# The first norm of a two-block transformer kernel: its modulation columns by pairs of pieces, the tiles behind them, two weight pieces over four PSUM banks

## What is computed

```python
c_act = silu(c)                                   # c: (1, 1024)
mod = (c_act @ w_ada[l] + b_ada[l]).reshape(B, 9, 1024)
sh1, sc1, gt1, ... = mod                          # shift, scale, gate, three times
hn = rms_norm(h, g_ffn1[l]) * (1.0 + sc1) + sh1
h = h + 0.5 * (1.0 + gt1) * swiglu(hn, w_ffn1_in[l], w_ffn1_out[l])
```

## Time and profile before

| | |
|---|---|
| median of 3 runs | 2898.18 us (2896.74 to 2901.25) |
| span of the profiled execution | 2894.2 us |
| the profiled execution's own time | not given apart from its span; the median is 3.98 us above the span |
| TensorE matmul busy | 2752.6 us, 95% of the span |
| VectorE busy | 1490.7 us, 52% |
| ScalarE busy | 967.7 us, 33% |
| GpSimd busy | 199.7 us, 7% |
| first matmul of an "up" piece | at 40.3 us |

### The profile page before, as it was taken

How to read it: one execution, slowest core, us unless ns; L and a number is a source line. 1 busy time by engine, 2 the same in 40 slices (tenths; PEclk the granted TensorE clock), 3 DMA queues, 4 the chain that set the end, 5 groups by cost and what they waited for, 6 DMA issues and landing times.

```text
span 2894.2 us, 42214 instructions
## 1 busy us (share of the span) xinstructions
PE 2752.6 (95%) x17756; PEld 2244.9 (78%) x17756; DVE 1490.7 (52%) x1833; ACT 967.7 (33%) x1471; POOL 199.7 (7%) x271
## 2 busy tenths in 40 slices
PE   6999999898999999999999899999999999968998
PEld 5888877686888878888777777888877777648787
DVE  6565566745555443333357634333365556656534
ACT  3222334523222233222345323222324444422322
POOL 3000000410000000000002300000010000013000
PEclk9999999989999999999999989999999999969999
DMA  7565542102566322232222012232222221100132
GB/s 287 197 226 205 184 160 77 44 18 85 206 205 216 103 94 102 84 112 81 101 73 74 6 59 76 91 103 97 99 89 72 81 73 66 62 1 4 56 102 73
DMA packets 46522, 299.68 MB, mean 104 GB/s; under 512 B 5665, under 2 KB 5793, under 8 KB 18081
## 3 DMA queue, kind: packets, MB, share of 16 engines
q1 hardware_dynamic: 37152, 230.35, 23.3%
q0 software_dynamic: 9216, 67.11, 6.4%
HBM read 295.35 MB, written 2.10 MB: 103 GB/s over the span
## 4 chain that ended last, share of the span: by engine, by line
PE 88%; DVE 8%; ACT 2%; DMA 1%; issue 1%; POOL 0%; SPq 0%; DVEq 0%; ACTq 0%; POOLq 0%
PE ps L920 17%; PE ps L921 17%; PE ps L922 17%; PE ps L1208 5%; PE ps L1209 5%; PE ps L1210 5%; PE ps L1515 2%; PE ps L1516 2%; PE ps L1517 2%; PE ps L2069 1%; PE ps L2053 1%; PE ps L2066 1%; DVE w_lo L897 1%; DMA ada_first<-in_ada 1%; PE ps L1330 1%; DVE tmp L876 1%
## 5 line engine op out<-in xcount | busy, mean ns | idle before, releaser
L920 PE MATMUL ps<-hn_hi,w_hi 128*128 128x512 f32 x1472 | 578.1, 393 | 26.0 <-DVE hn_lo L870 16.7
L921 PE MATMUL ps<-hn_lo,w_hi 128*128 128x512 f32 x1472 | 576.4, 392 | 0.0
L922 PE MATMUL ps<-hn_hi,w_lo 128*128 128x512 f32 x1472 | 575.8, 391 | 0.0
L897 DVE TENSOR_TENSOR w_lo<-w_raw,w_hi 128x2048 fp32r<-128x2048 f32 (+3 forms) x229 | 472.4, 2063 | 181.4 <-ACT w_hi L890 177.9
L890 ACT ACTIVATE w_hi<-w_raw 128x2048 fp32r<-128x2048 f32 (+3 forms) x229 | 394.5, 1723 | 115.8 <-PE ps L1210 97.3
L920 PEld LDWEIGHTS ps<-hn_hi,w_hi 128*128 128x128 f32 x1472 | 278.8, 189 | 87.6 <-issue 28.8
L1208 PE MATMUL ps<-hn_hi,w_hi 128*128 128x512 f32 x776 | 323.3, 417 | 7.8 <-DVE hn_lo L870 4.9
L922 PEld LDWEIGHTS ps<-hn_hi,w_lo 128*128 128x128 f32 x1472 | 278.7, 189 | 58.2
L921 PEld LDWEIGHTS ps<-hn_lo,w_hi 128*128 128x128 f32 x1472 | 279.0, 190 | 57.7
L1209 PE MATMUL ps<-hn_lo,w_hi 128*128 128x512 f32 x776 | 305.8, 394 | 0.0
L1210 PE MATMUL ps<-hn_hi,w_lo 128*128 128x512 f32 x776 | 305.4, 394 | 0.0
(11 more groups left out here) (462 smaller groups left out, 3499.0 us busy)
## 6 DMA issues: line engine op xcount, KB each, us to landing
w_raw<-in_up SPq DMA_DIRECT2D x88, 1024.0 KB, 4.9
ada_w<-in_ada POOLq DMA_DIRECT2D x64, 1024.0 KB, 5.2
w_raw<-in_down SPq DMA_DIRECT2D x64, 704.0 KB, 4.0
w_raw<-in_mix_in SPq DMA_DIRECT2D x20, 1024.0 KB, 4.9
w_raw<-in_dsa_in SPq DMA_DIRECT2D x18, 1024.0 KB, 4.9
w_raw<-in_merge SPq DMA_DIRECT2D x16, 768.0 KB, 4.3
ada_first<-in_ada SPq DMA_DIRECT2D x8, 1024.0 KB, 12.4
w_raw<-in_mix_out SPq DMA_DIRECT2D x8, 1024.0 KB, 5.0
```

The costliest lines, as they stand in the source:

```text
L897: dve.tensor_tensor(w_lo[:, slot, 0:size], w_raw[:, slot, 0:size], w_hi[:, slot, 0:size].bitcast(F32), ALU.subtract).then_inc(w_lo_ready, 1)
L920: pe.matmul(bank, wh, x_hi[:, k], start=(k == 0), stop=False)
L921: pe.matmul(bank, wh, x_lo[:, k], start=False, stop=False)
L922: return pe.matmul(bank, wl, x_hi[:, k], start=False, stop=(k == K - 1))
```

## The change

- **Loads.** x comes in two halves. The weights of piece 0 are issued ahead of the `ada` pieces, those of piece 1 after the first four of them. The `ada` pieces come as pairs: a scale piece, then the shift piece of the same two tiles (4, 0, 5, 1, 6, 2, 7, 3), from the third pair on each after the piece two pairs before. The weights of piece 2 are the next that the loop over weights issues.
- **Sum of squares.** The first norm adds six of its squared tiles on VectorE as the later norms do. The identity matrix has a mark of its own, so the spread no longer waits for the other masks.
- **Columns.** Of each piece, the first column stays one custom instruction on VectorE. For the second, GpSimd multiplies (128 x 1024, both inputs in SBUF), ScalarE sums with a Copy that has an accumulator, and VectorE adds the bias (one column).
- **Tiles.** `norm_gain` is formed column by column, and each tile's L876, `hn_hi` and `hn_lo` follow as soon as its two columns are there. VectorE finishes one tile (`low(j)`) before it goes on.
- **Pieces 0 and 1.** TensorE runs both while the tiles arrive: piece 0 in full for each k, piece 1's two products with `w_hi` from k = 3 on, and piece 1's sixteen products with `w_lo` last. The two pieces are in four banks. Splits: piece 1's inside the norm, piece 2's in step 0.
- **GpSimd.** The six levels of masks go out of `make_masks` into `level_masks`, behind the norm and between the first two later `ada` loads and the rest. Later marks count one higher.
- **Step 0.** The first later `ada` piece is summed after `act_lo`, not ahead of `act_f`.

```diff
-    sp.dma_start(h[:], w["x"]).then_inc(x_loaded, 16)
-    for q in range(ADA_FIRST):
-        if q == ADA_FIRST - 2:
-            sp.dma_start(w_raw[:, 0, 0:WIDE], w["up"]((0, 0), 0)).then_inc(raw_loaded[0], 16)
-        if q >= 4:
-            sp.wait_ge(ada_first_loaded[q % 4], 16)
-        sp.dma_start(ada_first[:, q], w["ada"][q]).then_inc(ada_first_loaded[q % 4], 16)
+    for q in range(X_PARTS):
+        part = slice(q * KD // X_PARTS, (q + 1) * KD // X_PARTS)
+        sp.dma_start(h[:, part], w["x"][:, part]).then_inc(x_loaded[q], 16)
+    sp.dma_start(w_raw[:, 0, 0:WIDE], w["up"]((0, 0), 0)).then_inc(raw_loaded[0], 16)
+    for pair in range(ADA_FIRST // 2):
+        for q in (ADA_FIRST // 2 + pair, pair):
+            if pair >= 2:
+                sp.wait_ge(first_loaded(q), 16)
+            sp.dma_start(ada_first[:, q], w["ada"][q]).then_inc(first_loaded(q), 16)
+        if pair == 1:
+            sp.dma_start(w_raw[:, 1, 0:WIDE], w["up"]((0, 0), 1)).then_inc(raw_loaded[1], 16)
...
-            if isinstance(i, int) and p0 + i == 0:
-                return
-            if not (isinstance(i, int) and p0 + i < 2):
-                sp.wait_ge(w_lo_ready, p0 + i - 1)
+            sp.wait_ge(w_lo_ready, p0 + i - 1)
...
+        elif p0 == 0:
+            steps(sp, n - 2, lambda i, odd: load(i + 2, odd))
...
        select(ident[:], [[-1, P]], 0, 1, ALU.not_equal, 1.0)
+        pool.memset(pool_mark[:], 0.0).then_inc(masks_ready, 1)
...
+    def level_masks(pool):
         for lv in range(1, 7):
...
-    pool.wait_ge(ada_done, ADA_FIRST)
-    load_ada(0, ADA_BEFORE_MIX)
+    pool.wait_ge(c_row_ready, 1)
+    for pair in range(ADA_FIRST // 2):
+        for q in (ADA_FIRST // 2 + pair, pair):
+            pool.wait_ge(first_loaded(q), 16 * (pair // 2 + 1))
+            pool.tensor_tensor(ada_first[:, q, 1], ada_first[:, q, 1], c_row[:], ALU.mult).then_inc(ada_multiplied, 1)
+    pool.wait_ge(hn_ready, KD)
+    load_ada(0, 2)
+    level_masks(pool)
+    load_ada(2, ADA_BEFORE_MIX)
...
+def first_column_dve(dve, own, q):
+    dve.wait_ge(first_loaded(q), 16 * (q % (ADA_FIRST // 2) // 2 + 1))
+    col = 2 * q
+    ws = ada_first[:, q, 0]
+    own(dve.tensor_tensor_reduce(ws, ws, c_row[:], 1.0, b_ada[:, col:col + 1], ALU.mult, ALU.add, mod[:, col:col + 1]))
+def second_column_dve(dve, own, q):
+    half_, pair = (0, q - ADA_FIRST // 2) if q >= ADA_FIRST // 2 else (1, q)
+    dve.wait_ge(ada_done, 2 * pair + half_ + 1)
+    col = 2 * q + 1
+    own(dve.tensor_tensor(mod[:, col:col + 1], mod[:, col:col + 1], b_ada[:, col:col + 1], ALU.add))
+def second_column_act(act, q):
+    half_, pair = (0, q - ADA_FIRST // 2) if q >= ADA_FIRST // 2 else (1, q)
+    act.wait_ge(ada_multiplied, 2 * pair + half_ + 1)
+    col = 2 * q + 1
+    act.activation(ada_first[:, q, 1], ada_first[:, q, 1], ACT.Copy, accum_out=mod[:, col:col + 1]).then_inc(ada_done, 1)
+def first_norm_act(act):
+    shift = mods(0, 0)
+    for j in range(KD):
+        pair, odd = j // 2, j % 2
+        second_column_act(act, ADA_FIRST // 2 + pair if odd == 0 else pair)
+        act.wait_ge(hn_tmp, j + 1)
+        act.activation(hn_hi[:, j], tmp[:, odd], ACT.Identity, bias=shift[:, j:j + 1]).then_inc(hn_hi_ready, 1)
+        if j == 3:
+            split_act(act, (1, 1), WIDE)
+def first_norm_dve(dve, own):
+    gain, shift, scale = gains[:, 0, 0], mods(0, 0), mods(0, 1)
+    def tile_(j):
+        own(dve.scalar_tensor_tensor(norm_gain[:, j:j + 1], scale[:, j:j + 1], 1.0, gain[:, j:j + 1], ALU.add, ALU.mult))
+        if j >= 2:
+            dve.wait_ge(hn_ready, j - 1)
+        dve.scalar_tensor_tensor(tmp[:, j % 2], h[:, j], norm_gain[:, j:j + 1], small[0], ALU.mult,
+                                 ALU.mult).then_inc(hn_tmp, 1)
+    def low(j):
+        dve.wait_ge(hn_hi_ready, j + 1)
+        dve.scalar_tensor_tensor(hn_lo[:, j], tmp[:, j % 2], shift[:, j:j + 1], hn_hi[:, j].bitcast(F32),
+                                 ALU.add, ALU.subtract).then_inc(hn_ready, 1)
+    first = ADA_FIRST // 2
+    for pair in range(first):
+        first_column_dve(dve, own, first + pair)
+        if pair:
+            second_column_dve(dve, own, first + pair - 1)
+            second_column_dve(dve, own, pair - 1)
+            tile_(2 * pair - 1)
+            low(2 * pair - 1)
+        first_column_dve(dve, own, pair)
+        if pair == 0:
+            dve.wait_ge(norm_spread, 1)
+        tile_(2 * pair)
+        low(2 * pair)
+        if pair == 2:
+            split_dve(dve, (1, 1), WIDE)
+    second_column_dve(dve, own, ADA_FIRST - 1)
+    second_column_dve(dve, own, first - 1)
+    tile_(KD - 1)
+    low(KD - 1)
...
+        act.wait_ge(sq_added, SQ_ADDS * n + max(1, j - 2))
...
+            if j % (KD // X_PARTS) == 0:
+                act.wait_ge(x_loaded[j * X_PARTS // KD], 16)
             norm_square(act, 0, j)
-    act.wait_ge(sq_summed, KD + 2 * n)
+    act.wait_ge(sq_summed, 2 * (n + 1))
...
+def first_pieces_pe(pe):
+    def products(p, t, k, low):
+        col = (2 * k + t) * P
+        wh, wl = w_hi[:, p, col:col + P], w_lo[:, p, col:col + P]
+        bank = main[p][t]
+        if low:
+            return pe.matmul(bank, wl, hn_hi[:, k], start=False, stop=(k == KD - 1))
+        pe.matmul(bank, wh, hn_hi[:, k], start=(k == 0), stop=False)
+        return pe.matmul(bank, wh, hn_lo[:, k], start=False, stop=False)
+    pe.wait_ge(w_lo_ready, 1)
+    for k in range(KD):
+        pe.wait_ge(hn_ready, k + 1)
+        for t in range(2):
+            products(0, t, k, False)
+            last = products(0, t, k, True)
+        if k == KD - 1:
+            last.then_inc(piece_done, 1)
+        if k == 3:
+            pe.wait_ge(w_hi_ready, 2)
+            for kk in range(3):
+                for t in range(2):
+                    products(1, t, kk, False)
+        if k >= 3:
+            for t in range(2):
+                products(1, t, k, False)
+    pe.wait_ge(w_lo_ready, 2)
+    for t in range(2):
+        for k in range(KD):
+            last = products(1, t, k, True)
+    last.then_inc(piece_done, 1)
...
-        norm_act_out(act, 0, mods(l, mi))
+        first_norm_act(act)
...
+            if p0 == 0 and isinstance(i, int) and i == 0:
+                split_act(act, (2, 0), WIDE)
+            elif not (p0 == 0 and isinstance(i, int) and i == 1):
+                split_act(act, *ahead(p0, HALF, WIDE, i, odd))
...
-            split_dve(dve, *ahead(p0, HALF, WIDE, i, odd))
-            if with_ada:
+            if not (p0 == 0 and isinstance(i, int) and i < 2):
+                split_dve(dve, *ahead(p0, HALF, WIDE, i, odd))
+            elif i == 0:
+                split_dve(dve, (2, 0), WIDE)
+            if with_ada and not (p0 == 0 and i == 0):
...
             dve.tensor_tensor(act_lo[:, bass.ds(i, 1), :], act_f[:, s:s + 1],
                               act_hi[:, bass.ds(i, 1), :].bitcast(F32), ALU.subtract).then_inc(dve_evac, 1)
+            if with_ada and p0 == 0 and i == 0:
+                dve_ada(dve, n0)
...
-    for j in range(KD):
-        norm_sum(pe, 0, j)
     pe.wait_ge(masks_ready, 1)
-    norm_spread_pe(pe, 0)
+    norm_sums(pe, 0)
...
-    for q in range(ADA_FIRST):
-        if q == ADA_FIRST - 3:
-            norm_dve_rstd(dve, own, 0)
-        if q == ADA_FIRST - 1:
-            split_dve(dve, (0, 0), WIDE)
-        dve_ada_first(dve, q)
-    dve.wait_ge(ada_done, ADA_FIRST)
+    for j in range(1, SQ_ADDS + 1):
+        norm_add(dve, 0, j)
+    norm_dve_rstd(dve, own, 0)
+    split_dve(dve, (0, 0), WIDE)
+    first_norm_dve(dve, own)
...
```

More of the change, by code:

```diff
@@ L102 @@
 SQ_ADDS = 5
+X_PARTS = 2
 VEC = {"mu": 8, "w0": 2, "a0": 2, "k_k": 2, "k_a": 2, "r_k": 2, "gn_w": 2, "gn_b": 2, "conv": 6, "q_gain": 1, "k_gain": 1}
@@ L481, in program @@
         small_loaded = sem("small_loaded")
-        x_loaded = sem("x_loaded")
+        x_loaded = [sem(f"x_loaded{q}") for q in range(X_PARTS)]
         c_row_loaded = sem("c_row_loaded")
@@ L515, in mods, with first_loaded @@
             return mod[:, at:at + KD]
+        def first_loaded(q):
+            pair, half_ = q % (ADA_FIRST // 2), q // (ADA_FIRST // 2)
+            return ada_first_loaded[2 * (pair % 2) + half_]
         def vcol(l, name, j=0):
@@ L621, in _, with compact @@
             nstep = [0]
+            full = restart[:, 0:P]
+            chunked = [[-HD, 2], [0, HD]]
+            def compact(which, scale=1.0):
+                pool.tensor_tensor(mask[:, which], full[:, 0:HD], full[:, HD:P], ALU.add).then_inc(mask_step, 1)
+                nstep[0] += 1
+                pool.wait_ge(mask_step, nstep[0])
+                if scale != 1.0:
+                    pool.tensor_scalar(mask[:, which], mask[:, which], scale, None, ALU.mult).then_inc(mask_step, 1)
+                    nstep[0] += 1
+                    pool.wait_ge(mask_step, nstep[0])
             def make_masks(pool):
-                chunked = [[-HD, 2], [0, HD]]
                 fill(ident[:], 0.0)
```

(20 more changed lines are left out.)

39 lines of the change are left out of this document (20 added, 19 removed).

## The result

| | before | after |
|---|---|---|
| median of 4 runs, us | 2898.0 (2896.7 to 2901.3) | 2924.8 (2919.0 to 2925.9) |
| span of the profiled execution, us | 2894.2 | 2923.8 |
| mean granted clock of TensorE | 0.968 | 0.962 |

The ratio is 1.0086, with a 95% interval of 1.0070 to 1.0101: slower by 20.3 to 29.3 us, 24.9 at the middle. The forecast was 2917.2 with a range of 2906 to 2924. The direction and the mechanism came as forecast. By the two medians the kernel is 26.8 us slower, and 2924.8 lies 7.6 us above the forecast and 0.8 above the range; by the ratio it is 24.9 above 2898.2, that is 2923.1, just inside.

The account below looks back on a forecast made before the run. TensorE bounds the kernel (88% of the 2894.2 us span); only the start changes. Piece 4 begins 17.4 us later, plus 1.6 for the clock: +19.0, 2913.2 against the span, 2917.2 for the median, 3.98 above; range 2906 to 2924.

Parts of the forecast that it names:

- series work of VectorE: In the first norm, VectorE's own columns, tiles, one-column instructions and piece 1's low split run in series: 35.0 us.
- products in the way: In the first norm, GpSimd's products and VectorE's two-input instructions exclude each other, costing VectorE 14.4 us.
- T: End of the first norm, when the eighth tile (its `hn_lo`) is ready: forecast at 69.7 us.
- masks: Behind the norm, GpSimd makes six mask levels ahead of issuing the third later `ada_w` piece: 19.5 us.
- restart, in piece 4: After a gap of over 4 us before piece 4, TensorE restarts at half rate, costing 1.6 us.
- Up to the first column: Start: loads, squares and token sums done at 15.9 us, piece 0's low split through at 20.3, then first column.
- (A): Rival, products in the way in part: one-column instructions don't wait, masks take 15.3 us, no clock-slowing gap; +10.9, 2909.1; chance 0.15.
- From T to piece 4: Piece 2 starts at T + 7.6, third later piece lands at T + 26.0, piece 4 starts 7.8 later at 103.5.
- The sum as an end-to-end time: Whole program: piece 4's delay of +17.4 plus 1.6 for the clock passes on as +19.0 us.
- (B): Rival: GpSimd's eight products never in VectorE's way in the norm; T = 55.3, total -1.3, 2896.9; chance 0.08.
- (C): Rival: start really gained, VectorE keeps up with landing; T near 41.8, total -10, 2888; chance 0.05.
- (D): Rival: in the norm TensorE waits for tiles nearly all the time, so four banks do nothing; no time or chance of its own.

Follow-up runs that it names:

- e8_one_input: After with GpSimd's products replaced by a multiplication by 1.0 with one SBUF input, leaving c out of the second columns; 2916.0 us, ratio 1.0062.
- e2_masks_spread: After with one level of GpSimd's masks behind each of the third to eighth later ada loads, instead of all six before the third; 2921.4 us, ratio 1.0056.
- e3_two_banks: After with pieces 0 and 1 run one behind the other, two banks at a time, as before the change; 2926.4 us, ratio 1.0075.
- e4_before_late: Before, with nothing of the change, plus nine further low splits of piece 0 on VectorE ahead of the first; 2922.3 us, ratio 1.0066.
- e1_no_product: After with each of GpSimd's eight products replaced by a one-element memset, so second columns are summed without c; 2916.3 us, ratio 1.0040.
- e5: After with each tile's `hn_lo` deferred behind VectorE's next first column or bias add; 2918.6 us, ratio 1.0060.
- e6: After without GpSimd products: VectorE sums all sixteen columns, masks back at their old place, gains paired, splits and low parts reordered; 2900.8 us, ratio 0.9999.

## Why the prediction was right, and where it was off

| step | predicted | after |
|---|---|---|
| first piece landed | 15.5 | 17.1 |
| token sums done | 15.9 | 20.9 |
| low split of piece 0 done, without products | 20.3 | 25.2 |
| series work of VectorE | 35.0 | 34.1 |
| products in the way | 14.4 | 10.0 |
| T | 69.7 | 69.3 |
| piece 2 starts | 77.3 | 77.7 |
| masks | 19.5 | 19.0 |
| third later piece landed | 95.7 | 95.8 |
| piece 4 starts | 103.5 | 103.9 |
| restart, in piece 4 | 1.6 | 1.9 |
| distance to before, past piece 4 | +19.0 | +19.7 |

**Up to the first column: wrong by 4.9 us.** I had "TensorE's three rounds of four small matmuls (0.2 us apart)". The first add comes at 10.99: half of x landed at 9.6 us, not 8.1. Why is not shown; in e8_one_input, with the same loads ahead of it, it landed at 8.45, so over a microsecond of this differs between executions. And each round is eight records of 0.22 us, not four: 24 of them take 5.27 us where I had 2.4. Before's timeline had them, 64 records for 32 blocks of squares; the earlier trace rows gave the duration of one and I took the count from the code. So the sqrt came at 20.9 instead of 16.

**Series work: right.** 34.1 us against 35.0, counted from the split's nominal end at 25.2 to T less 10.0.

**Products: right mechanism, 4.4 us too much.** I had charged seven products, two to eight. As VectorE began its split at 22.99 instead of 18.1, product two was through and three half done (1.3 us). Of the five others, four cost 2.0 to 2.1 us where I had 2.2 to 2.4, and one 0.5, and no bias add was met. The weakest assumption held: the one-column gain, for which no row existed, lasted 2.17 us instead of 0.16. (A) falls on this. The rule of the Trainium skill, page "SBUF — State Buffer", section "Who interferes with whom", that the first instruction to come keeps the port pair until it is through, agrees with these six. It does not fit e8_one_input, where a GpSimd instruction of 2.8 us that reads and writes SBUF held VectorE for 0.6 to 0.8; there the measurement decides.

**T itself: right by cancellation.** +4.9, -0.9 and -4.4 give -0.4.

**From T to piece 4: right.** Every station of it, T + 7.6, the masks of 19.5, T + 26.0 and 7.8 behind it, came within 0.8 us. e2_masks_spread shows the masks' part by itself: 6.3 us of the distance, the restart in piece 4 included, but also 1.6 us because piece 2 ran at full rate there.

**The clock: one restart too few, without effect.** I had one, for the gap before piece 4. After has two. The one in piece 2 cost 1.9 us, and the wait for the third `ada_w` piece took it up; e3_two_banks has neither, and is 2.0 us earlier at piece 4. Half rate within the norm, until 57.1 us, fell into waits as I had it: pieces 0 and 1 ended at 75.6, the time in the sum.

**The sum as an end-to-end time: 5.9 us short.** At pieces 6 to 38 the sum is right to 0.7 us. The measured ratio makes it 24.9 (20.3 to 29.3). In the profiled pair another 10.3 us arise past 410 us, in few steps. They come with a lower clock: after's is 0.93, 0.88, 0.92, 0.88 and 0.84 in the five stretches between the columns of the table, before's 0.94, 0.91, 0.94, 0.91 and 0.87. What lowered it is not shown. 4.3 of the 10.3 lie past 2495. All eight other kernels fall back there against before, by 2.9 to 10.4 us, e4_before_late by 7.4 with nothing of the change. So a loss of this size there needs nothing of the change; before's one profiled run was quicker in that stretch than any other. My range allowed nothing for such wandering. Whether a part of the other 6.0 us is the change's own is not settled. Between 410 and 790 us after and e1 to e3 lose 2.7 to 4.4 us and e5 0.5, while e4 wins 2.5, e6 2.4 and e8 1.6. As e6 and e8 have most of the change in their later norms too, nothing in it can be named as the cause, and intervals of 4 us to either side don't tell it apart.

**The rivals.** (A) falls: one-column instructions wait, the masks took 19.0, and there are gaps that slow the clock. (B) falls with e1_no_product. (C) falls: even with no products T was 59.3, and with VectorE never held up 51.7, against the 41.8 that (C) needs; the series work binds, as the earlier trace rows said. (D) holds in its result, four banks gain nothing, but TensorE was busy for 24.3 of 35 us; its reason falls.

Of 19.7 us, then, e1 takes away 10.1, e2 6.3 and e5 5.2, each from after alone. They were not run together, and need not add up.

## What to carry to other kernels

Work moved to a second engine is only off the first if both can reach memory at once: look in the trace for any pair of the two that overlaps, and charge what such a pair shows: here nearly the whole of the second engine's instruction if it had two inputs, a quarter of it with one. When a step is moved behind another one on an engine's queue, ask what else that queue issues behind it, here the third load behind six levels of masks. And count the records of a wait in the timeline, not the calls in the code.
